# Score products of four key pages, cut into two parts of two pages each, in a one-core decode and prompt step

## The chip, the cores and the metric

One core of a Trainium2 chip. The metric is the device time of one launch in microseconds; lower is better.

## The reference, cut to what matters

One layer of a hybrid decoder for a prompt of 16 + 256 tokens and for 8 decode sequences of 4 new tokens each. Every decode sequence has 2048 past tokens in 16 pages of 128 tokens, in a paged cache of keys and values (float32, 1024 numbers per token each). What the change touches is the product of the queries with the past keys:

```python
q, k, v, u = project_in(xs, l, attn_norm, w_in, q_norm, k_norm)
k_past = cache_k[l][page_table].reshape(db, past_len, 2 * N_HEADS, HEAD_DIM)
v_past = cache_v[l][page_table].reshape(db, past_len, N_HEADS, 2 * HEAD_DIM)
o = diff_attn_core(q, k_all, v_all, q_pos, k_pos, lam)   # softmax over all keys, two maps, values
```

Around it stand the input projection (2048 x 5120), a convolution group, the output projection (2048 x 2048) and an MLP (2048 x 8192 and back), all in float32.

## The kernel before, in words

A weight matrix goes in **visits** of 512 output columns; a visit has 8 chunks of 512 KB (`raw`), which ScalarE rounds to `w_hi` (L1124) and VectorE turns into a rest `w_lo` (L1454). TensorE makes three products of 128x128 tiles for each of 16 row tiles (L691 to L693). The input projection has 10 visits.

**The paged attention runs beside these visits.** Each engine has a program of its own, written out by hand as a `body` of 16 **slots** per decode sequence (the loops over `j`). In the body that works on the keys of sequence `ks` it also works on the values of sequence `vs`, the one before, and on visit `n` of the input projection. There is one body with keys alone (ks=0), then five with keys, values and a visit (ks=1 to 5, called the visit bodies below; the variable `s` of these loops is vs=0 to 4), then two with keys and values beside the prompt's attention and no visit (ks=6 and 7, the free bodies), and a last one for the values of sequence 7. After that come the output projection and the MLP, which is all of the second half of the time.

**A key page's way.** GpSimd (POOL) loads it: `load_keys` (L572 to L579) reads the page number, waits, and issues four DMAs of 128 KB into slot `j % 8` of `k_page`. VectorE transposes it in place in blocks of 32 (`turn`, L1532 to L1536, semaphore `kt_ok`), two slots of the program ahead of need in a visit body (`TURNS`), four ahead in a free body (`FREE_TURNS`). TensorE multiplies a **group** of four pages with the queries of the sequence (`score`, L768 to L780): 8 calls of 512 columns into the one PSUM bank `aux[:, 0]`, then `sc_mm` rises by one. ScalarE copies the bank to `s_rows` (`take_scores`, L1175 to L1181) and raises `s_ev`, which the next group's product waits for. VectorE takes the group's maximum (L1621). At the end of a body come the whole maximum (L1629, L1631), the exponentials on ScalarE (L1218), and in `fresh` (L1609) the next sequence's queries in `q_cur` (L1541) and its products with the new keys in `s_cur` (L1588).

`k_page` has room for 8 pages, so page `j` of a sequence may be loaded only when the page 8 before it has been multiplied. Before, POOL waits for the whole group of four that was two groups earlier. The groups' slots are 3, 7, 11, 15 in a visit body (`SCORES`), 0, 4, 8, 12 in a free body (`FREE_SCORES`), and 5, 10 for groups 2 and 3 of sequence 0 (`FIRST_SCORES`); groups 0 and 1 of sequence 0 come inside visit 3.

On TensorE a slot is, in this order: the group's product if it has one, `new_keys` (L805 to L820, in slot 1 of most bodies), the visit's twelve products of one row tile, `turn_probs` (L792 to L803: transposes of the exponentials of sequence `vs`, slots 0 to 3; the transposes of slots 1 and 3 are copied by VectorE at L1640), and `values` (L822 to L846) of page `j - 2`. The queue of SyncE (SP) loads the chunks of the weights (L392, when TensorE has used an earlier one) and the pages of values (L418, when TensorE has used an earlier one). POOL has three more tasks in between: convolution taps (L619, L621) and outputs (L587, L593, L595) in the fourth visit body and around it, and value outputs (L604).

Of the kernel before, what the change touches and what calls it, by code (L numbers as in the profile page):

```python
# [14 lines left out]
P = 128  # L15
# [5 lines left out]
N_SEQ = 8  # L21
# [14 lines left out]
N_PAGES = 16  # L36
# [9 lines left out]
QD = 32  # L46
NB = P // QD
# [3 lines left out]
SG = 4  # L51
KS = 2 * SG
NG = N_PAGES // SG
# [57 lines left out]
def build_step(nc, x_prompt, x_sample, cache_k, cache_v, state_conv, page_table, meta_tokens,  # L111
# [4 lines left out]
    with ctx:  # L116
# [12 lines left out]
        def sem(name):  # L129
            return ctx.enter_context(nc.semaphore(name))  # L130
# [91 lines left out]
        aux = ctx.enter_context(nc.psum_tensor("aux", [P, 4, 512], F32))  # L222
# [44 lines left out]
        kt_ok = sem("kt_ok")  # L267
        qs_ok = sem("qs_ok")
        qc_ok = sem("qc_ok")
        sc_mm = sem("sc_mm")  # L270
        s_ev = sem("s_ev")
# [85 lines left out]
        def key_rows(r, b):  # L357
            return k_pages[ds(r, 1)].rearrange("a (q x) (b e) -> (a x) q b e", x=KX, b=NB)[:, :, b, :]


        def last_values(i):
            return k_page[:, i % KS].rearrange("p g q c -> p (g q c)")
# [11 lines left out]
        def key_quarter(slot, b):  # L374
            return k_page[QD * b:QD * (b + 1), slot].rearrange("p g q c -> p g (q c)")
# [5 lines left out]
        def _(sp):  # L381
# [15 lines left out]
            def load_last(i):  # L397

                s = N_SEQ - 1
                r = sp.value_load(pages_sb[0:1, ds(N_PAGES * s + i, 1)], min_val=0, max_val=n_phys - 1)  # L400
                src = v_pages[ds(r, 1)].rearrange("a p n -> p (a n)")
                if i >= KS:
                    sp.wait_ge(pv_mm, VR + N_PAGES * s + i - KS + 1)
                elif i < VR:
                    sp.wait_ge(pv_mm, N_PAGES * s + i + 1)
                else:
                    sp.wait_ge(sc_mm, NG * N_SEQ)
                if i % KS < VR:
                    sp.dma_start(v_page[:, i % VR], src).then_inc(v_in[i % VR], 16)
                else:  # L410
                    sp.dma_start(last_values(i), src).then_inc(vk_in[i % VR], 16)
# [57 lines left out]
            for i in range(VR):  # L469
                load_last(i + VR)  # L470
# [2 lines left out]
            for i in range(KS, N_PAGES):  # L473
                load_last(i)

            sp.wait_ge(sc_mm, NG * N_SEQ)
            sp.dma_start(x_nat[:, 0, :], xp[0:P, :]).then_inc(x2_in[0], 16)
            sp.dma_start(x_nat[:, 1, :], xp[P:2 * P, :]).then_inc(x2_in[1], 16)
            sp.wait_ge(pt_mm, NG * N_SEQ)
# [16 lines left out]
            for g in range(4):  # L496
                cols = slice(VC * g, VC * (g + 1))
# [16 lines left out]
        def _(pool):  # L514
# [51 lines left out]
            ks = k_sample[0].rearrange("b t h d -> (b t) (h d)")  # L566
# [5 lines left out]
            def load_keys(s, j, used=True):  # L572

                r = pool.value_load(pages_sb[0:1, ds(N_PAGES * s + j, 1)], min_val=0, max_val=n_phys - 1)  # L574
                slot = j % KS
                if used:
                    pool.wait_ge(sc_mm, NG * s + j // SG - 1)
                for b in (0, 2, 1, 3):
                    pool.dma_start(key_quarter(slot, b), key_rows(r, b)).then_inc(k_in[slot], 16)  # L579

# [91 lines left out]
        def _(pe):  # L672
            mm, transpose = nc.tensor.matmul, nc.tensor.transpose
# [53 lines left out]
            for kt in range(KT):  # L727
# [4 lines left out]
                if kt == 3:  # L732

                    pe.wait_ge(state_in, STATE)
                    for c in range(8):
                        last = transpose(aux[:, 2, TAPS * c:TAPS * (c + 1)], cw_nat[:, P * c:P * (c + 1)],
                                         ident[0:TAPS, 0:TAPS])
# [7 lines left out]
                if kt == 13:  # L745

                    pe.wait_ge(set_v, 14)
                    for t, (t0, n) in enumerate(TOK):
                        last = mm(aux[:, 3, t0:t0 + n], rb[0:n, t, :], ident[0:n, 0:n], start=True, stop=True)
# [15 lines left out]
                    if kt == 3:  # L765
                        norm_sums(n)

            def score(s, g):  # L768

                pe.wait_ge(kt_ok, N_PAGES * s + SG * (g + 1))  # L770
                if g == 0:
                    pe.wait_ge(qc_ok, (NB + 1) * s + NB)
                pe.wait_ge(s_ev, NG * s + g + 2)
                keys = k_page[:, SG * (g % 2):SG * (g % 2 + 1)].rearrange("p j g q c -> p (j g) q c")
                for half in range(2):
                    for c in range(NB):
                        last = mm(aux[QD * c:QD * (c + 1), 0, :].rearrange("p (k c) -> p k c", c=QD),  # L777
                                  q_cur[:, 2 * c + half, :], keys[:, :, 2 * c + half, :],
                                  start=(half == 0), stop=(half == 1))
                last.then_inc(sc_mm, 1)  # L780

            for kt in range(KT):
                products(EARLY, kt, a_hi, a_lo, 0, T)
# [8 lines left out]
            def turn_probs(s, g):  # L792

                pe.wait_ge(exp_ok, (NG + 1) * s + g + 1)
                if g % 2 == 0:
                    pe.wait_ge(pt_d, 1 + 2 * s + g // 2)
                else:
                    pe.wait_ge(pt_a, 2 * s + g // 2 + 1)
                pe.sem_inc(pe_go, 1)
                for j in range(SG):  # L800
                    last = transpose(aux[:, 2, P * j:P * (j + 1)], s_rows[:, P * (SG * g + j):P * (SG * g + j + 1)],  # L801
                                     ident[:])
                last.then_inc(pt_mm, 1)  # L803

            def new_keys(vs, ks):  # L805

                pe.wait_ge(o_ok, (vs if vs is not None else 0) + 1)
                if vs is not None:
                    pe.wait_ge(exp_ok, (NG + 1) * (vs + 1))
                    pe.wait_ge(sel_v, 3 * (vs + 1))  # L810
                    pe.sem_inc(pe_go, 1)
                    mm(aux[0:N_SMP, 3, C_AN:C_AN + 2 * HR], s_rows[:, PAST:PAST + N_SMP],
                       pick_s[:].rearrange("p a c -> p (a c)"), start=True, stop=True)
                    mm(aux[:, 3, C_PV:C_PV + 2 * HR], perm[:].rearrange("p b x c -> p (b x c)"),
                       pick_s[:].rearrange("p a c -> p (a c)"), start=True, stop=True).then_inc(an_mm, 1)
                if ks is not None:
                    pe.wait_ge(qc_ok, (NB + 1) * (ks + 1))
                    pe.sem_inc(pe_go, 1)
                    transpose(aux[:, 3, C_SN:C_SN + N_SMP], s_cur[:].rearrange("p a c -> p (a c)"),
                              ident[0:N_SMP, 0:N_SMP]).then_inc(sn_t, 1)  # L820
# [27 lines left out]
            def body(ks, vs, n, middle=None, end=None, finish=None, new_at=1, scores=SCORES):  # L848


                for j in range(N_PAGES):
                    if ks is not None and j in scores:
                        score(ks, scores[j])
                    if j == new_at:
                        new_keys(vs, ks)
                    if middle:
                        middle(j)
                    if n is not None:
                        products(n, j, a_hi, a_lo, 0, T)
                    if vs is not None and j < NG:  # L860
                        turn_probs(vs, j)
                    if j >= 2 and vs is not None:
                        values(vs, j - 2, ks is not None)
                    if end:
                        end(j)
                if vs is not None:
                    values(vs, N_PAGES - 2, ks is not None)
                    values(vs, N_PAGES - 1, ks is not None)
                    if finish:
                        finish()  # L870

                    pe.wait_ge(or_ok, vs + 1)
                    for a in range(2):
                        last = mm(aux[:, 3, C_EX + HR * a:C_EX + HR * (a + 1)], o_rows[:, P * a:P * (a + 1)],
                                  pick_v[:, a, :], start=True, stop=True)
                    last.then_inc(ex_mm, 1)
# [46 lines left out]
            for t0, n in NAT:  # L923
                for half in range(2):
                    if b >= 4:
                        pe.wait_ge(nat_d if half else nat_a, b // 2 - 1)
                    for h in range(4):
                        last = transpose(acc[0:n, b % 4, P * h:P * (h + 1)],
                                         z[:, 16 + 4 * half + h, PAD + t0:PAD + t0 + n], ident[:])
# [177 lines left out]
            for g in range(4):  # L1107
                pe.wait_ge(acc_free, MT + MT * (MLP_V0 + N_QTR * QTR_N - DOWN_N + g + 1))
                for i, (t0, n) in enumerate(TOK_OUT):
# [3 lines left out]
                    for m in range(MT):  # L1113
                        last = transpose(aux[0:n, b % 4, P * m:P * (m + 1)], xT[:, MT * g + m, t0:t0 + n], ident[:])
# [3 lines left out]
        def _(act):  # L1118
# [55 lines left out]

            def take_scores(ks, g, vs=None):  # L1175

                act.wait_ge(sc_mm, NG * ks + g + 1)
                if vs is not None:
                    act.wait_ge(pt_mm, NG * vs + g + 1)
                nc.scalar.copy(s_rows[:, SG * P * g:SG * P * (g + 1)].rearrange("p (j y g x) -> p j y g x", j=SG, y=KY, g=NB),  # L1180
                               aux[:, 0, :].rearrange("p (j g x y) -> p j y g x", j=SG, g=NB, x=KX)).then_inc(s_ev, 1)  # L1181
# [252 lines left out]
            for b in range(0, 12, 2):  # L1434
                g, i = b // 3, b % 3
# [7 lines left out]
        def _(dve):  # L1443
# [164 lines left out]

            def fresh(ks):  # L1609

                dve.wait_ge(sc_mm, NG * ks)
                dve.wait_ge(sn_t, ks)
                copy_queries(ks)
                copy_new(ks)
# [381 lines left out]
            for b in range(1, 12, 2):  # L1996
                g, i = b // 3, b % 3
# [31 lines left out]
```

## Time and profile before

| what | us |
|---|---|
| median of 3 runs | 1622.88 (1622.68 to 1639.64) |
| the profiled execution, its own time | 1632.08 |
| span of the profiled execution | 1630.4 |
| TensorE busy | 1514.5 (93% of the span) |
| VectorE busy | 975.2 (60%) |
| POOL, DMA issues of the key pages | 332.1, 512 of them |

The profile page is of one execution. Its second section cuts the span into 40 slices of 40.8 us; the keys' loads lie in slices 2 to 16, and from about 690 us on the kernel is the output projection and the MLP. Share of DMA is that of the core's 16 DMA engines.

### The profile page before, as it was taken

The page shows a single profiled execution, that of the slowest core. Times are in us where ns is not written, and L with a number is a line of the kernel's source. Part 1 is how long each engine was busy: PE and PEld are TensorE (multiplying, and loading weights), DVE is VectorE, ACT ScalarE, POOL GpSimd, SP SyncE. Part 2 cuts the span into 40 slices and gives each one's busy share as a digit, 9 for nine tenths or more (in the row PEclk, how much of TensorE's full clock was granted, in tenths as well). Part 3 has the DMA queues.
Part 4 walks back from the last instruction along what each step waited for, and adds up shares of the span by engine and source line. Part 5 has one row for each costly group of instructions (what it writes and reads, how often), then busy time and mean ns, then how long its engine had stood idle before and what let it go on. Part 6 is the DMA issues. An engine that isn't in the chain of part 4 may idle for free.

```text
span 1630.4 us, 31305 instructions
## 1 busy us (share of the span) xinstructions
PE 1514.5 (93%) x11203; PEld 1348.6 (83%) x11203; DVE 975.2 (60%) x1469; ACT 593.8 (36%) x929; POOL 419.7 (26%) x656
## 2 busy tenths in 40 slices
PE   5999898797877868899999999999999999999998
PEld 5988766565654433599999999999999999999998
DVE  3689857998998775353645544455444554445444
ACT  4433312122222332443544433443334433344432
POOL 4597656765787653000000000000000000000000
PEclk9999998998997977799999999999999999999999
DMA  7746799999999776834555545555455545555444
GB/s 201 215 144 185 234 321 333 353 341 327 342 305 349 252 236 221 289 118 154 155 158 165 168 167 162 164 165 166 167 166 162 164 165 167 167 163 163 165 166 148
DMA packets 163845, 340.50 MB, mean 209 GB/s; under 512 B 33915, under 2 KB 33971, under 8 KB 163168
## 3 DMA queue, kind: packets, MB, share of 16 engines
q1 hardware_dynamic: 120592, 267.29, 51.1%
q0 software_dynamic: 43168, 72.15, 14.5%
q8 instruction: 45, 0.74, 0.2%
q14 instruction: 40, 0.33, 0.1%
HBM read 334.00 MB, written 5.96 MB: 209 GB/s over the span
## 4 chain that ended last, share of the span: by engine, by line
PE 72%; issue 10%; DVE 7%; DMA 5%; POOL 3%; POOLq 2%; ACT 1%; SPq 0%; ACTq 0%
PE acc L691 21%; PE acc L693 21%; PE acc L692 21%; DMA k_page<-in_cache_k 3%; PE aux L777 2%; DVE k_page L1536 2%; POOL k_page L579 1%; PE aux L842 1%; POOLq L574 1%; DVE w_lo L1454 1%; DMA raw<-in_w_in 1%; PE acc L945 1%; PE aux L801 1%; POOLq L579 1%; PE acc L965 1%
## 5 line engine op out<-in xcount | busy, mean ns | idle before, releaser
L1454 DVE TENSOR_TENSOR w_lo<-raw,w_hi 128x1024 fp32r<-128x1024 f32 x368 | 451.5, 1229 | 410.2 <-ACT w_hi L1124 409.3
L691 PE MATMUL acc<-a_hi,w_hi 128*128 128x288 f32 (+1 forms) x1920 | 591.8, 308 | 35.2 <-DVE w_lo L1454 26.4
L1124 ACT CAST w_hi<-raw 128x1024 fp32r<-128x1024 f32 x368 | 384.9, 1049 | 586.5 <-DMA raw<-in_w_down 255.4
L693 PE MATMUL acc<-a_hi,w_lo 128*128 128x288 f32 (+1 forms) x1920 | 578.4, 301 | 0.0
L692 PE MATMUL acc<-a_lo,w_hi 128*128 128x288 f32 (+1 forms) x1920 | 578.2, 301 | 0.0
L691 PEld LDWEIGHTS acc<-a_hi,w_hi 128*128 128x128 f32 x1920 | 367.6, 191 | 72.5 <-DVE w_lo L1454 36.5
L579 POOL DMA_DIRECT2D k_page<-in_cache_k x512 | 332.1, 649 | 204.5 <-issue 89.3
L692 PEld LDWEIGHTS acc<-a_lo,w_hi 128*128 128x128 f32 x1920 | 368.3, 192 | 0.5
L693 PEld LDWEIGHTS acc<-a_hi,w_lo 128*128 128x128 f32 x1920 | 368.4, 192 | 0.0
L693 PE MATMUL acc<-h_hi,w_lo 128*128 128x288 f32 x1024 | 302.2, 295 | 0.0
L692 PE MATMUL acc<-h_lo,w_hi 128*128 128x288 f32 x1024 | 301.5, 294 | 0.0
L691 PE MATMUL acc<-h_hi,w_hi 128*128 128x288 f32 x1024 | 301.1, 294 | 0.0
L691 PEld LDWEIGHTS acc<-h_hi,w_hi 128*128 128x128 f32 x1024 | 192.1, 188 | 0.0
L693 PEld LDWEIGHTS acc<-h_hi,w_lo 128*128 128x128 f32 x1024 | 192.1, 188 | 0.0
L692 PEld LDWEIGHTS acc<-h_lo,w_hi 128*128 128x128 f32 x1024 | 192.1, 188 | 0.0
L1536 DVE STREAM_TRANSPOSE k_page<-k_page 128x1024 f32<-128x1024 f32 x128 | 156.8, 1231 | 31.7 <-DMA k_page<-in_cache_k 31.2
L1602 DVE SCALAR_TENSOR_TENSOR conv<-z,taps,conv 128x256 f32<-128x256 f32 x240 | 100.3, 477 | 0.1
L777 PE MATMUL aux<-k_page,q_cur 128*32 128x512 f32 x512 | 70.8, 676 | 20.8 <-DVE k_page L1536 13.8
L1180 ACT COPY s_rows<-aux 128x512 f32<-128x512 f32 x32 | 18.8, 588 | 167.0 <-PE aux L777 167.0
L842 PE MATMUL aux<-v_page,pT 128*16 128x256 f32 x960 | 77.7, 409 | 1.6 <-DMA v_page<-in_cache_v 1.6
L777 PEld LDWEIGHTS aux<-k_page,q_cur 128*32 128x32 f32 x512 | 16.7, 122 | 55.5 <-issue 33.1
L1913 DVE TENSOR_TENSOR xT<-xT,acc 128x288 f32 (+1 forms) x80 | 32.9, 454 | 46.3 <-PE acc L693 46.3
(224 smaller groups left out, 892.6 us busy)
## 6 DMA issues: line engine op xcount, KB each, us to landing
k_page<-in_cache_k POOLq DMA_DIRECT2D x512, 128.0 KB, 6.6
raw<-in_w_up SPq DMA_DIRECT2D x128, 512.0 KB, 3.7
raw<-in_w_down SPq DMA_DIRECT2D x128, 512.0 KB, 3.6
v_page<-in_cache_v SPq DMA_DIRECT2D x120, 512.0 KB, 7.6
raw<-in_w_in SPq DMA_DIRECT2D x80, 512.0 KB, 6.0
raw<-in_w_out SPq DMA_DIRECT2D x32, 512.0 KB, 3.7
k_page<-in_cache_v SPq DMA_DIRECT2D x8, 512.0 KB, 5.5
x_nat<-in_x_prompt SPq DMA_DIRECT2D x3, 1024.0 KB, 8.9
```

The lines of the kernel that those rows point to most:

```text
L579: pool.dma_start(key_quarter(slot, b), key_rows(r, b)).then_inc(k_in[slot], 16)
L691: mm(out, wh, ah, start=(kt == 0), stop=False)
L692: mm(out, wh, al, start=False, stop=False)
L693: last = mm(out, wl, ah, start=False, stop=(kt == KT - 1))
L777: last = mm(aux[QD * c:QD * (c + 1), 0, :].rearrange("p (k c) -> p k c", c=QD), q_cur[:, 2 * c + half, :], keys[:, :, 2 * c + half, :], st ...
L842: last = mm(aux[QD * b:QD * b + HR, 3, 0:2 * P].rearrange("p (a c) -> p a c", a=2), pT[:, b, j, :], page[:, 2 * P * b:2 * P * (b + 1)].rea ...
L1124: nc.scalar.copy(w_hi[:, j % RAW], raw[:, j % RAW]).then_inc(hi_ok, 1)
L1180: nc.scalar.copy(s_rows[:, SG * P * g:SG * P * (g + 1)].rearrange("p (j y g x) -> p j y g x", j=SG, y=KY, g=NB), aux[:, 0, :].rearrange("p ...
L1454: v.tensor_tensor(w_lo[:, j % RAW], raw[:, j % RAW], w_hi[:, j % RAW].bitcast(F32), ALU.subtract)\
L1536: v.transpose(keys, keys).then_inc(kt_ok, 1)
L1602: v.scalar_tensor_tensor(dst, src, w, dst, ALU.mult, ALU.add).then_inc(cv_p, 1)
L1913: v.tensor_tensor(x, x, acc[:, m, 0:T_OUT], ALU.add).then_inc(acc_free, 1)
```

## The change

A group's product is cut in two parts: part 0 multiplies the group's first two pages into the first 256 columns of the bank, part 1 the other two into the last 256. Part 1 stays in the slot of the group, part 0 comes two slots before it (in slot 0 both stand together, since there is no earlier slot; the same in `score`, for groups 0 and 1 of sequence 0). Each part raises `sc_mm` by one, so all waits on it count double. POOL waits for the part that held the page 8 before, no longer for the group.

```diff
-                    sp.wait_ge(sc_mm, NG * N_SEQ)
+                    sp.wait_ge(sc_mm, 2 * NG * N_SEQ)
...
-                    pool.wait_ge(sc_mm, NG * s + j // SG - 1)
+                    pool.wait_ge(sc_mm, 2 * NG * s + (j - KS) // 2 + 1)
...
-            def score(s, g):
-
-                pe.wait_ge(kt_ok, N_PAGES * s + SG * (g + 1))
-                if g == 0:
-                    pe.wait_ge(qc_ok, (NB + 1) * s + NB)
-                pe.wait_ge(s_ev, NG * s + g + 2)
-                keys = k_page[:, SG * (g % 2):SG * (g % 2 + 1)].rearrange("p j g q c -> p (j g) q c")
+            def score_part(s, g, x):
+
+                pe.wait_ge(kt_ok, N_PAGES * s + SG * g + SG // 2 * (x + 1))
+                if x == 0:
+                    if g == 0:
+                        pe.wait_ge(qc_ok, (NB + 1) * s + NB)
+                    pe.wait_ge(s_ev, NG * s + g + 2)
+                j0 = SG * (g % 2) + SG // 2 * x
+                keys = k_page[:, j0:j0 + SG // 2].rearrange("p j g q c -> p (j g) q c")
+                cols = slice(2 * P * x, 2 * P * (x + 1))
                 for half in range(2):
                     for c in range(NB):
-                        last = mm(aux[QD * c:QD * (c + 1), 0, :].rearrange("p (k c) -> p k c", c=QD),
+                        last = mm(aux[QD * c:QD * (c + 1), 0, cols].rearrange("p (k c) -> p k c", c=QD),
                                   q_cur[:, 2 * c + half, :], keys[:, :, 2 * c + half, :],
                                   start=(half == 0), stop=(half == 1))
                 last.then_inc(sc_mm, 1)
+
+            def score(s, g):
+                for x in range(2):
+                    score_part(s, g, x)
...
                 for j in range(N_PAGES):
                     if ks is not None and j in scores:
-                        score(ks, scores[j])
+                        if j == 0:
+                            score_part(ks, 0, 0)
+                        score_part(ks, scores[j], 1)
+                    if ks is not None and j + 2 in scores:
+                        score_part(ks, scores[j + 2], 0)
...
-                act.wait_ge(sc_mm, NG * ks + g + 1)
+                act.wait_ge(sc_mm, 2 * (NG * ks + g + 1))
...
-                dve.wait_ge(sc_mm, NG * ks)
+                dve.wait_ge(sc_mm, 2 * NG * ks)
```

## Rows read from the trace of the kernel before

**Rows 1.** The page's second section: busy tenths in 40 slices, the clock and the DMA.

```profile
POOL 4597656765787653000000000000000000000000
PEclk9999998998997977799999999999999999999999
DMA  7746799999999776834555545555455545555444
```

**Rows 2.** Waits between 60 and 640 us: total, times, longest.

```profile
POOL k_page L579 <- PE aux L777: 71.5, 16, 10.2
DVE k_page L1536 <- DMA k_page<-in_cache_k: 31.2, 28, 3.2
PE aux L777 <- DVE k_page L1536: 12.8, 9, 8.5
DVE w_lo L1454 <- ACT w_hi L1124: 25.0, 14, 5.7
```

**Rows 3.** Windows, one per body: length, engines' busy time, TensorE clock, DMA share, GB/s.

```profile
200.00:262.00 62.00, 51.17 (x407) 36.03 (x405) 34.13 (x46) 14.45 (x26) 38.15 (x60) 0.94 0.99 331
262.00:327.00 65.00, 54.68 (x425) 39.16 (x425) 59.70 (x113) 16.87 (x31) 44.83 (x70) 0.91 1.02 342
327.00:391.50 64.50, 53.98 (x425) 38.09 (x425) 62.74 (x121) 15.40 (x27) 43.22 (x69) 0.92 1.02 345
391.50:458.00 66.50, 54.08 (x426) 38.56 (x426) 62.09 (x113) 17.09 (x31) 44.16 (x70) 0.91 1.00 331
458.00:523.00 65.00, 53.41 (x409) 37.34 (x409) 61.13 (x117) 13.68 (x25) 49.10 (x78) 0.89 0.98 319
523.00:595.00 72.00, 56.89 (x377) 30.44 (x377) 55.65 (x119) 30.49 (x100) 44.94 (x71) 0.85 0.79 256
595.00:645.00 50.00, 42.66 (x252) 19.24 (x252) 31.07 (x74) 15.61 (x62) 23.54 (x37) 0.78 0.78 246
```

**Rows 4.** Windows of 5 us, the same columns.

```profile
185.00:190.00 5.00, 5.00 (x64) 3.32 (x64) 0.62 (x1) 0.27 (x1) 0.25 (x1) 0.94 0.44 114
...
230.00:235.00 5.00, 5.00 (x48) 3.65 (x40) 2.62 (x3) 1.05 (x1) 3.37 (x6) 1.00 1.04 358
```

**Rows 5.** Timeline of POOL: start, length, line, count, in brackets the idle time before and its releaser.

```profile
190.44 1.99 POOL L579 DMA_DIRECT2D k_page<-in_cache_k  x3 [5.19 <-PE aux L777]
...
214.62 2.66 POOL L579 DMA_DIRECT2D k_page<-in_cache_k  x4 [10.24 <-PE aux L777]
217.98 2.66 POOL L579 DMA_DIRECT2D k_page<-in_cache_k  x4 [0.70 <-issue]
...
405.09 2.67 POOL L579 DMA_DIRECT2D k_page<-in_cache_k  x4 [9.68 <-PE aux L777]
...
631.14 2.68 POOL L579 DMA_DIRECT2D k_page<-in_cache_k  x4 [1.76 <-PE aux L777]
```

**Rows 6.** Timeline of TensorE, the same columns.

```profile
204.61 0.22 PE L812 MATMUL aux<-pick_s,s_rows 128*32 128x32 f32 x2 [2.31 <-DVE pick_s L1689]
...
257.51 1.55 PE L842 MATMUL aux<-v_page,pT 128*16 128x256 f32 x24
...
273.78 1.90 PE L777 MATMUL aux<-k_page,q_cur 128*32 128x512 f32 x16
275.61 0.66 PE L913 MATMUL aux<-ident,z 128*128 128x128 f32 x4
...
534.00 3.47 PE L777 MATMUL aux<-k_page,q_cur 128*32 128x512 f32 x16 [2.80 <-DVE s_cur L1588]
537.41 0.66 PE L801 MATMUL aux<-ident,s_rows 128*128 128x128 f32 x4
```

**Rows 7.** Timeline of VectorE, the same columns.

```profile
243.89 1.25 DVE L1536 STREAM_TRANSPOSE k_page<-k_page 128x1024 f32<-128x1024 f32 x1 [3.19 <-DMA k_page<-in_cache_k]
...
265.78 0.86 DVE L1541 COPY q_cur<-q_sel 32x32 f32<-32x32 f32 x4
...
271.31 0.42 DVE L1640 COPY pT<-aux 128x256 f32<-128x256 f32 x1 [2.18 <-PE aux L801]
```

More of the change, by code:

```diff
@@ L474, in _ @@
                 load_last(i)
-            sp.wait_ge(sc_mm, NG * N_SEQ)
+            sp.wait_ge(sc_mm, 2 * NG * N_SEQ)
             sp.dma_start(x_nat[:, 0, :], xp[0:P, :]).then_inc(x2_in[0], 16)
```

## The prediction, made before the changed kernel was run

> **What bounds the kernel now.** I began with the 40 slices. From slice 18 on DMA is at four to five tenths and POOL idle: the second half is weight products and holds no key load [rows 1]. Whatever the change does happens before 690 us, and a gain there shifts the rest of the program as a whole. In slices 7 to 13 DMA shows nine tenths. Next the waits between 60 and 640 us. POOL stood 71.5 us on 16 score products: that is what the change aims at. But the engines that use the pages lost less: VectorE waited 31.2 us for key pages to land, TensorE's scores 12.8 us for VectorE's transposes [rows 2]. So at most some 31 us of POOL's 71.5 is felt downstream directly, and the question is what stands behind.
>
> The windows by body say it. Where DMA is full its share reads 1.04, at 358 GB/s [rows 4]. The first visit body (200 to 262 us) reads 0.99, the others 1.02, 1.02, 1.00 and 0.98 [rows 3]. All five are within 6% of a full DMA. Their bytes are fixed: 16 key pages, 16 value pages and 8 chunks of 512 KB, 40 x 0.524 = 21.0 MB, which takes 59.6 us at 352 GB/s (between the 342 of a body and the 358 of the full window). The bodies take 62 to 66.5 us. In four of them VectorE is busy 60 to 63 of some 65 us besides [rows 3], so both limits lie close under the present time. In the two free bodies DMA reads 0.79 and 0.78, and VectorE 56 of 72 and 31 of 50 us: here neither is full, and the chain of the prompt's attention goes from engine to engine.
>
> **The change part by part.**
>
> *Earlier release of key pages in the visit bodies.* In the first visit body POOL finishes page 7 at 204.4 us and stands 10.24 us until group 0 is done at 213.8 [rows 5]. Part 0 will stand in slot 1, ahead of `new_keys`, whose first product started at 204.61 [rows 6]. I put its end at 206.3, so page 8 is issued at about 207 in place of 214.6, 7.6 us earlier; pages 10 and 11 need part 1, which still ends near 214, and POOL gets there at 207 + 2 x 3.36 = 213.7 (3.36 is 217.98 less 214.62 [rows 5]). So nearly all of the stall goes. The same holds in the other visit bodies (5.99, 7.87 and 9.68 us of stall in the second to the fourth; in the fifth POOL is late by its own taps and outputs and does not stand).
>
> What that is worth is bounded by DMA. If only DMA's unfilled time can be won, that is (1.05 - share)/1.05 x length: 3.5, 1.9, 1.8, 3.2 and 4.3 us, together 14.7 us [rows 3]. I take these terms down where VectorE binds too. First body: VectorE has 34 of 62 us busy and waited there ten times for key pages, 21.4 us in all, of which the row of 243.89 is one [rows 7]; nothing but DMA binds, and ahead of it DMA is far from full (0.44 in 185 to 190 us [rows 4]) while POOL stood 5.19 us for group 3 of sequence 0 [rows 5], whose part 0 moves from slot 10 to slot 8. Filling that moves four pages up by some 4.5 us. I take 5 us here. Second body 1, third 0.5 (VectorE 62.7 of 64.5 busy), fourth 2, fifth 2.5. Sum 11 us. Bounds: 2 us (VectorE's order alone decides after the first body and the first gets only its 2) and 20 us (a whole stall of POOL per body at the places where VectorE waits, 21.4 us in the first and about 7 in the rest, less what DMA refuses).
>
> *Part 0 in slot 1 of a visit body.* It is queued before `new_keys`, the visit's products of that slot, and `turn_probs` of slot 1, for which VectorE waits at L1640 (2.18 us at 271.31 [rows 7]). It needs the queries, ready at 265.78 + 0.86 = 266.64 [rows 7], about when `new_keys` began anyway, and the start of a body is where the clock is down: a group took 3.47 us at 534.00 at 1.2 GHz against 1.90 at full clock [rows 6]. So part 0 puts 1.0 to 1.8 us in front of VectorE's wait. In the second and fourth body VectorE has later waits of the same slots that take most of it up (0.85 and 0.46 us, and 0.86 us); in the third and the fifth there is 0.2 to 0.6 us of slack. At slot 3 TensorE has it back, since part 1 is half a group. Price: 0.5 us a body, 2.5 us in all; bounds 0 and 5 x 1.8 = 9 us.
>
> *More instructions.* A group was 16 recorded matmuls of 512 columns, 1.83 us from its start to the next operation's (275.61 less 273.78 [rows 6]). The rate for 256 columns is that of the value products: 24 in 1.55 us, less a last one of about 0.38, is 0.051 us each [rows 6]. 16 of them are 0.82 us, plus about 0.15 to enter and leave the narrow tiling (8 of them took 0.56 where the rate gives 0.41). Two parts: 1.94 us, +0.11 a group, +3.3 us over 30 groups on an engine that waits at every body's end. I count 0.5 us; bounds 0 and 3.3. The Trainium skill (TensorEngine Tiling (Array Packing), Key Properties) says that changing the tiling mode drains TensorE, and the change doubles the number of such changes; the 0.15 us above is what the trace shows for one, and by it the sum stays as it is.
>
> *The free bodies.* Both parts of group 0 stand in slot 0, but pages 8 and 9 go when part 0 is done: 3.47/2 = 1.7 us earlier. The third stall of length is 6.57 us at 585.5, where VectorE's layer norm of slot 10 held page 15's transpose; part 0 of group 3, in slot 10, needs pages 12 and 13 only and is past that. The last page was issued at 631.14 after stalls of 3.69, 4.66 and 1.76 us in its body [rows 5]; POOL should now reach it 6 to 9 us earlier. Downstream, though, VectorE waited for landings only 0.66, 0.42 and 1.66 us in 534 to 645, and TensorE's one long wait (8.5 us [rows 2]) is for page 15's transpose, which does not move. Gain 2.7 us of landings, plus 1.7 us because at the last group half of the product is done before. Less 1 us for parts put in front of the prompt's products: 3.4 us, say 3. Bounds 0 and 12.
>
> *Waits on `sc_mm` of SP, ScalarE and VectorE* are for the same moment, the end of a group's part 1: nothing. The wait on `s_ev` comes two slots earlier, but ScalarE copies a group 0.6 us after it ends and the next part 0 is two slots away: nothing.
>
> *Sum:* 11 - 2.5 - 0.5 + 3 = 11 us. The profiled execution took 1632.1 us, 9.2 above the median of the runs shown; 1621 against it is 1612 against the median of 1622.9.
>
> **Rivals.**
>
> *POOL's rate is the true bound.* From the first to the fourth visit body each page 8 follows the last by 54 us of issuing and 6 to 10 of standing; the period is that sum. If DMA's full share in the trace is only the queue built up after each late start, then the stalls come off the period: 10 + 6 + 8 + 10 less the 2.5 us above, and 6 of the free bodies' 27, some 35 us at most. Against it stand 59.6 us of bytes per body and a busy VectorE. As a case I take 25 us: 1598.
>
> *It is hidden almost wholly.* VectorE binds from the second body on, and the free bodies wait on the prompt's chain. Then only the first body's 4 us less 2 to 3 us of part 0 remains: 1621. For it: busy times of 60 to 63 us. Against: VectorE waited for key landings near the end of each of these bodies, and again for the weights.
>
> *Slower: keys in front of weights.* At a body's start TensorE waits for `w_lo`, VectorE for `w_hi` (25.0 us, 14 times [rows 2]), ScalarE for raw chunks. Now key pages and the chunks of slots 2 to 4 are loaded at one time, where before POOL stood. If four DMAs of keys (two pages, 1.05 MB, 3 us at 352 GB/s) come before a chunk, VectorE's order slips by up to 3 us in a body that it binds; with the 1.8 us of part 0 that is 4.8 us x 5 = 24, less the 11: 13 us slower, 1636. It decides if the chunk's landing was the last thing VectorE waited for at the body's start, which it was in three bodies by 0.85 to 1.75 us. The Trainium skill (DMA: Bandwidth & Descriptors, Queues, rings and completion order) states that each DMA engine takes turns between the queues that have work, packet by packet. By that rule a chunk loses part of its rate while keys are queued, not its whole place; this leaves the rival with half its price. No row shows single packets here.
>
> **How the numbers follow.** Forecast (about 11 us, own range 1605 to 1618): 0.50. POOL's rate (1598): 0.20. Hidden (1621): 0.22. Slower (1636): 0.08. The range 1597 to 1624 leaves out the slower case and the end of the POOL case. One per cent, 16.2 us, is about what a measurement of this kernel can tell from no change. Faster by more than that (under 1606.7) is the POOL case and a little of the forecast's upper end: 0.26. Slower by more is the outer half of the last rival: 0.05. Within 1%: 0.69.
>
> **What would show it.** Right: POOL's wait for L777 falls from 71.5 to under 25 us; in the first visit body page 8 is issued near 207 and VectorE's waits for landings, 21.4 us, fall by a third or more; DMA shares of the visit bodies go to 1.03 and over; bodies of 60 to 64 us; the score of a part near 1.0 us at full clock; the last score about 11 us earlier and everything after it unchanged in length. The POOL rival: bodies under 59 us. The hidden rival: POOL's wait gone and bodies two to five the same. The slower one: more time of ScalarE on `raw` and of VectorE on `w_hi` in slots 2 to 4, or on L801. The forecast is wrong if the bodies after the first do not shorten, or if a new stall of POOL on later parts takes the old one's place with the same length.

## The result, and the profile of the changed kernel

| what | before | changed |
|---|---|---|
| median of 20 runs, us | 1626.57 (1621.71 to 1639.64) | 1617.35 (1615.61 to 1622.91) |
| profiled execution, span, us | 1630.4 | 1615.0 |

The ratio is 0.994, 95% interval 0.9926 to 0.9954: 9.2 us faster by the medians. In the comparisons below the ratios leave out one run of `early_both` and one of the kernel before beside it, which took several times as long as the rest. The two profiled spans differ by 15.4 us, more than the medians; part of that is chance, as a second trace of the kernel before shows below.

The page's second section, against [rows 1]: the work of the first third is packed a little closer, the second half is the same.

```profile
POOL 4498667766776752000000000000000000000000
PEclk9999999998988969799999999999999999999999
DMA  7656899999999868645555555555555555555554
```

The waits between 60 and 640 us, against [rows 2] (total, times, longest; L781 is now the score product, L1548 the transpose, L850 the product with the values, L1652 the copy of transposed probabilities):

```profile
ACT w_hi L1136 <- DMA raw<-in_w_in: 101.7, 35, 6.8
...
POOL k_page L579 <- PE aux L781: 52.2, 15, 12.6
...
DVE w_lo L1466 <- ACT w_hi L1136: 27.1, 16, 4.6
...
PEld aux L850 <- DMA v_page<-in_cache_v: 22.3, 13, 3.3
PE aux L781 <- DVE k_page L1548: 20.4, 22, 8.0
...
PE aux L850 <- DMA v_page<-in_cache_v: 16.7, 11, 2.8
...
DVE pT L1652 <- PE aux L809: 11.7, 6, 4.4
...
DVE k_page L1548 <- DMA k_page<-in_cache_k: 9.3, 5, 2.5
```

POOL's wait for scores fell only from 71.5 to 52.2 us; in the five visit bodies alone it fell from 37.3 (200 to 523 us) to 31.4 (200 to 514 us). VectorE's wait for key pages fell from 31.2 to 9.3. What is new is TensorE waiting for **value** pages: 13 waits, 22.3 us, at the weight loads and 16.7 at the matmuls of much the same stops; before there were 5, of 3.6 us in all. ScalarE's wait for chunks of the weights (`raw`) rose too, from 76.7 us in 24 waits to 101.7 in 35. Keys that come earlier are paid for with values and weights that come later.

Windows by body, against [rows 3]. Body ends are read at the last small product of a body, which before stood at 262.3, 327.1, 391.6, 457.9, 523.3, 594.9 and 660.0 us and now at 261.1, 323.4, 386.6, 451.1, 513.8, 587.2 and 639.1.

```profile
200.00:261.00 61.00, 50.37 (x460) 36.61 (x458) 32.77 (x45) 16.90 (x34) 38.88 (x60) 0.93 0.97 324
261.00:323.40 62.40, 53.06 (x489) 39.34 (x489) 58.80 (x113) 14.23 (x21) 44.70 (x70) 0.94 1.05 354
323.40:386.60 63.20, 53.16 (x489) 38.56 (x489) 62.48 (x120) 15.65 (x27) 43.19 (x67) 0.93 1.05 352
386.60:451.00 64.40, 53.11 (x489) 39.24 (x489) 60.42 (x112) 16.79 (x31) 44.28 (x71) 0.92 1.03 346
451.00:513.80 62.80, 52.90 (x473) 37.74 (x473) 61.17 (x119) 14.27 (x25) 48.43 (x77) 0.91 0.98 325
513.80:587.20 73.40, 59.80 (x440) 33.87 (x440) 55.36 (x118) 31.59 (x102) 45.20 (x71) 0.81 0.86 271
587.20:639.00 51.80, 44.98 (x389) 22.89 (x389) 35.05 (x87) 19.55 (x79) 20.72 (x32) 0.93 0.76 248
```

The second to the fourth visit body now have DMA at 1.05, 1.05 and 1.03, where it was 1.02, 1.02 and 1.00; 1.05 is the highest share that any of these traces reads over a body. They are 62.4, 63.2 and 64.4 us long, the fifth 62.8 at an unchanged 0.98. The first visit body ended only 1.2 us earlier, and its share is 0.97. In windows of 5 us, against [rows 4]:

```profile
205.00:210.00 5.00, 5.00 (x29) 4.38 (x22) 1.66 (x2) 0.00 (x0) 2.59 (x4) 0.50 0.82 293
210.00:215.00 5.00, 5.00 (x47) 4.06 (x46) 2.12 (x6) 1.48 (x3) 2.59 (x4) 0.87 0.81 245
215.00:220.00 5.00, 5.00 (x48) 4.02 (x50) 5.00 (x6) 2.31 (x3) 3.67 (x6) 1.00 0.74 219
```

DMA is still not full from 205 to 220 us, and no fuller than before: the kernel before read 1.05, 0.75 and 0.63 in the same three windows, 0.81 in the mean beside 0.79 now (0.93 and 0.69 in the second traces, below). What was filled lies ahead of them: 185 to 190 us read 0.44 before and 0.61 now, 190 to 195 us 0.58 and 0.89. POOL's timeline, against [rows 5], says when pages 8 and 10 of that body and page 8 of the next were issued:

```profile
206.80 2.66 POOL L579 DMA_DIRECT2D k_page<-in_cache_k  x4 [8.10 <-PE aux L781]
...
215.55 2.66 POOL L579 DMA_DIRECT2D k_page<-in_cache_k  x4 [2.73 <-PE aux L781]
...
267.91 2.66 POOL L579 DMA_DIRECT2D k_page<-in_cache_k  x4 [3.08 <-PE aux L781]
```

Page 8 came at 206.8, as forecast (207), in place of 214.6; the stall was 8.10 us all the same, because POOL had been brought forward in the body before (it had finished page 7 at 198.7 us in place of 204.4). TensorE's and VectorE's timelines at the same place, against [rows 6] and [rows 7]:

```profile
204.27 1.78 PE L781 MATMUL aux<-k_page,q_cur 128*32 128x256 f32 x16 [3.11 <-issue]
205.74 0.32 PE L820 MATMUL aux<-pick_s,s_rows 128*32 128x32 f32 x2
```

```profile
272.49 1.05 PE L781 MATMUL aux<-k_page,q_cur 128*32 128x256 f32 x16
273.47 0.66 PE L925 MATMUL aux<-ident,z 128*128 128x128 f32 x4
```

```profile
211.09 0.42 DVE L1652 COPY pT<-aux 128x256 f32<-128x256 f32 x1 [4.44 <-PE aux L809]
...
240.45 1.25 DVE L1548 STREAM_TRANSPOSE k_page<-k_page 128x1024 f32<-128x1024 f32 x1 [2.55 <-DMA k_page<-in_cache_k]
...
253.20 1.25 DVE L1548 STREAM_TRANSPOSE k_page<-k_page 128x1024 f32<-128x1024 f32 x1 [2.00 <-DMA k_page<-in_cache_k]
```

A part takes 1.78 us in slot 1, where the clock is down, and 1.05 us at full clock, 0.98 to the start of the next operation (forecast 1.0 at full clock and 1.7 at the start of a body). `new_keys` comes 1.1 us later, and VectorE's first wait for transposed probabilities is 4.44 us where it was 1.85 in that body.

### The profile page after: what moved, and what is told of

Same layout as the page of the kernel before. It is cut to its first block, busy times and chain, and to the rows that moved or that the text cites. A ratio compares the mean times of both kernels' runs of the same rounds, so it can differ in the third digit from the quotient of the medians.

```text
span 1615.0 us, 32337 instructions
## 1 busy us (share of the span) xinstructions
PE 1507.7 (93%) x11715; PEld 1357.5 (84%) x11715; DVE 972.6 (60%) x1469; ACT 595.8 (37%) x929; POOL 420.5 (26%) x656
## 4 chain that ended last, share of the span: by engine, by line
PE 76%; DVE 18%; DMA 3%; issue 1%; ACT 1%; POOL 1%; SPq 0%; POOLq 0%; ACTq 0%
PE acc L691 22%; PE acc L693 21%; PE acc L692 21%; DVE conv L1614 6%; DVE k_page L1548 5%; DVE w_lo L1466 3%; PE aux L781 2%; PE aux L850 2%; DMA v_page<-in_cache_v 1%; PE acc L957 1%; PE acc L977 1%; PE aux L809 1%; DMA raw<-in_w_in 1%; DVE s_max L1633 1%; DVE z L1584 1%
## 5 line engine op out<-in xcount | busy, mean ns | idle before, releaser
L1548 DVE STREAM_TRANSPOSE k_page<-k_page 128x1024 f32<-128x1024 f32 x128 | 156.2, 1229 | 9.3 <-DMA k_page<-in_cache_k 9.3
L781 PE MATMUL aux<-k_page,q_cur 128*32 128x256 f32 x1024 | 72.4, 406 | 31.2 <-DVE k_page L1548 20.4
L850 PE MATMUL aux<-v_page,pT 128*16 128x256 f32 x960 | 78.9, 410 | 16.7 <-DMA v_page<-in_cache_v 16.7
L781 PEld LDWEIGHTS aux<-k_page,q_cur 128*32 128x32 f32 x1024 | 31.5, 114 | 63.3 <-DVE k_page L1548 32.5
```

Source lines behind the costliest of these rows:

```text
L781: last = mm(aux[QD * c:QD * (c + 1), 0, cols].rearrange("p (k c) -> p k c", c=QD), q_cur[:, 2 * c + half, :], keys[:, :, 2 * c + half, :], ...
L850: last = mm(aux[QD * b:QD * b + HR, 3, 0:2 * P].rearrange("p (a c) -> p a c", a=2), pT[:, b, j, :], page[:, 2 * P * b:2 * P * (b + 1)].rea ...
L1548: v.transpose(keys, keys).then_inc(kt_ok, 1)
```

## The experiments

Each ratio is to the kernel before, timed on the same chip. The column of the visit bodies is the distance from the first body's end to the fifth's in the trace of the run: the time that the change is about, free of what comes before and after. The last column is from the fifth body's end to the end of the last body.

| kernel | median, us | ratio (95%) | first body ends | visit bodies 2 to 5 | free and last bodies |
|---|---|---|---|---|---|
| before | 1626.57 | 1 | 262.3 | 261.0 | 164.3 |
| before_trace | 1619.65, one run | | 260.3 | 261.7 | 152.5 |
| changed | 1617.35 | 0.994 (0.9926 to 0.9954) | 261.1 | 252.8 | 158.4 |
| again_after | 1618.2 | 0.9926 (0.9901 to 0.995) | 264.2 | 253.0 | 157.7 |
| group_release | 1628.14 | 0.9991 (0.9971 to 1.0011) | 264.4 | 259.7 | 160.3 |
| same_slot | 1626.4 | 0.9973 (0.9947 to 0.9999) | 262.3 | 261.4 | 160.7 |
| late_first_part | 1622.74 | 0.9956 (0.9932 to 0.998) | 261.9 | 256.3 | 160.8 |
| visit_only | 1615.67 | 0.9925 (0.99 to 0.995) | 262.8 | 252.8 | 154.1 |
| free_only | 1628.04 | 1.001 (0.9988 to 1.0032) | 262.2 | 260.8 | 159.7 |
| early_queries | 1618.56 | 0.9928 (0.9904 to 0.9951) | 262.6 | 257.5 | 158.2 |
| early_both | 1624.79 | 0.9983 (0.9955 to 1.0011) | 258.3 | 258.7 | 161.2 |
| half_values_before | 1612.17 | 0.9883 (0.9822 to 0.9943) | 257.4 | 251.7 | 156.6 |
| half_values_after | 1609.13 | 0.9873 (0.9818 to 0.9929) | 253.8 | 253.6 | 158.6 |

**The two kernels once more.**

> The changed kernel once more, as the yardstick for the runs beside it: ratio to before 0.994 +- 0.002, as in the first measurement. Its trace should show again that the visit bodies end some 9 us earlier than before and tell how much of the free bodies' shift (13 us less in the second, 6 more in the last) is the clock of TensorE and not the change.

> The kernel before once more, for a second trace: the first one was 5 us above its median. If TensorE's half clock between 605 and 620 us was chance, the second free body ends 3 to 8 us earlier here and the difference to the changed kernel's trace at 640 us falls from 21 to some 10 us.

The changed kernel repeats itself: 253.0 us for the four bodies against 252.8. The second trace of the kernel before has a span of 1618.0 us, below all its timed medians; its visit bodies take 261.7 us, as in the first, but its free and last bodies are 11.8 us shorter. Its second free body ended 14.0 us earlier (646.0 beside 660.0 us), where 3 to 8 had been expected. Windows of the first trace (16 us) and then of the second (5 us each, the first and the last of four; all four read 1.00), the last columns being TensorE's clock, DMA's share and GB/s:

```profile
600.00:616.00 16.00, 16.00 (x80) 8.72 (x76) 9.76 (x26) 4.74 (x19) 10.36 (x16) 0.61 0.73 205
```

```profile
600.00:605.00 5.00, 4.83 (x35) 3.45 (x37) 4.02 (x11) 2.51 (x10) 4.25 (x8) 1.00 0.48 128
...
615.00:620.00 5.00, 4.02 (x30) 1.86 (x30) 4.90 (x11) 1.74 (x8) 3.69 (x7) 1.00 0.93 304
```

The first trace ran that stretch at a clock of 0.61 of full speed in the mean, the second at 1.00. The kernel was the same. So the last column of the table carries some 10 us of chance, a single pair of traces says nothing on the free bodies, and the 13 us that the second free body seemed to win are mostly this. By the five bodies' end the two traces of the kernel before stood at 523.3 and 522.1 us, those of the changed kernel at 513.8 and 517.2: 4.9 to 9.5 us, with the 9.2 of the medians inside. The spread comes from the end of the first visit body; the four bodies after it agree within 1 us from trace to trace of a kernel. That holds for their sum and not for a single one: the second body took 64.8 and 62.2 us in the two traces of the kernel before.

What the four bodies gain shows at VectorE. Its waits for key pages to land came there to 7.1 and 5.3 us in the two traces of the kernel before; in both traces of the changed kernel there is none. That is most of the 8 us.

**The release alone, and the lead alone.**

> The products stay in two parts at the new places, but POOL waits for whole groups again. Theory (the gain is the earlier release of pages): no gain is left and part 0 still stands in front of the body's start, so 0 to 3 us slower than before, ratio 1.000 to 1.002. Rival (the gain is that part 1 is only half a group on TensorE's path): most of the gain stays, ratio 0.995 to 0.997.

```diff
-                    pool.wait_ge(sc_mm, 2 * NG * s + (j - KS) // 2 + 1)
+                    pool.wait_ge(sc_mm, 2 * (NG * s + j // SG - 1))
```

> Both parts in the group's own slot, POOL waits for parts. Pages 8 and 9 are released 1 us earlier than in the kernel before and not 7 to 8. Theory (two slots of lead carry the gain): about before, ratio 0.998 to 1.000. Rival (release by halves is enough): ratio 0.994 to 0.996.

```diff
                     if ks is not None and j in scores:
-                        if j == 0:
-                            score_part(ks, 0, 0)
-                        score_part(ks, scores[j], 1)
-                    if ks is not None and j + 2 in scores:
-                        score_part(ks, scores[j + 2], 0)
+                        score(ks, scores[j])
```

With the products split and placed as in the change but the pages released by groups, nothing is left of the gain: 0.9991, visit bodies 259.7 us, and 4.6 us of waits for landings in them are back. So it does not come from a shorter last product on TensorE's path. Nor does TensorE's clock tell the kernels apart: over the first 16 us of each of the four bodies it was 0.82 in the mean here, 0.83 and 0.75 in the two traces of the kernel before, 0.84 in the changed kernel. Its windows are those of the kernel before [rows 3]; DMA's shares are back at 1.02, 1.03, 1.00 and 0.98; the second and the fourth body:

```profile
264.40:327.60 63.20, 52.76 (x490) 39.12 (x490) 59.25 (x112) 16.86 (x31) 43.46 (x68) 0.93 1.02 339
...
391.80:457.70 65.90, 53.62 (x490) 39.37 (x490) 61.05 (x112) 16.85 (x31) 44.30 (x71) 0.91 1.00 332
```

Nor does it show a cost of the 8 further matmul calls per group: the interval, 0.9971 to 1.0011, holds no change. With release by halves but no lead (`same_slot`) the visit bodies take 261.4 us with 6.6 us of waits for landings, as before; the ratio, 0.9973, lies a little under the range set down (0.998 to 1.000) and its interval ends just under 1, so a gain of some microseconds outside these bodies is not ruled out. For the visit bodies both halves of the change are needed: the product must come earlier and POOL must be let go by it.

**Where in the program.**

> The two free bodies work as before (both parts in the group's slot, POOL waits for whole groups for their pages), the visit bodies as in the changed kernel. The forecast's terms put 8 of 11 us into the visit bodies: with 9.5 us measured, 7 us faster than before, ratio 0.995 to 0.9965. If the free bodies carry the gain, as the two profiles side by side could be read (13 us less in the second free body), ratio 0.998 to 1.000.

> The counterpart: visit bodies as before, free bodies as in the changed kernel. Forecast's terms: 2 to 3 us faster than before, ratio 0.998 to 0.999. If the free bodies carry the gain: 7 us or more, ratio under 0.996.

In these two, `body` calls `score` for the bodies that stay as before, and `load_keys` waits by groups for the pages that those bodies set free. All of the gain is in the visit bodies (0.9925, 252.8 us; more than the 7 us expected), none in the free ones (1.001, where 0.998 to 0.999 was expected). `visit_only` has the lowest median of the kernels that do all the work, but its interval is that of the changed kernel; the two were not timed on one chip, and I don't call it faster. POOL did gain time in the free bodies of the changed kernel, as its timeline shows:

```profile
592.85 2.67 POOL L579 DMA_DIRECT2D k_page<-in_cache_k  x4 [12.63 <-PE aux L781]
```

POOL runs ahead through sequence 6 and then stands 12.63 us before page 8 of sequence 7, whose part 0 needs that sequence's queries, and these come at the body's end. The stalls of 6.57 and 3.69 us before pages 4 and 8 became one, those of 4.66 and 1.76 us before pages 12 and 15 went. The last page was issued 29.7 us after the start of its body (616.88 less 587.2), 6.5 us sooner than before (631.14 less 594.9), and in the trace of `free_only` VectorE never waits for a landing in the free bodies, where the kernel before did for 2.7 and 3.8 us in its two traces. So the pages came earlier as forecast and the time did not follow: they were not what these bodies waited for. What is, these runs don't show.

**Part 0 in front of the body's start.**

> Part 0 of group 0 in the visit bodies goes behind the products and the transposes of slot 1, so VectorE's first wait for transposed probabilities is as before, while pages 8 and 9 are released some 4 us later than in the changed kernel. If part 0 in front costs what the forecast took (0.5 us a body) or more and POOL's release is not the limit: 1 to 5 us faster than the changed kernel, ratio 0.991 to 0.9935. If the release time rules: 1 to 4 us slower than it, ratio 0.9945 to 0.9965.

```diff
                     if vs is not None and j < NG:
                         turn_probs(vs, j)
+                    if ks is not None and vs is not None and j == 1 and j + 2 in scores:
+                        score_part(ks, scores[j + 2], 0)
```

(and the call ahead of the products is left out for that slot.) The release time rules: 0.9956, visit bodies 256.3 us, 3.5 more than in the changed kernel. Page 8 was issued 2.8 to 5.7 us later after the start of its body than in the changed kernel (second to fourth visit body). Its waits, in the columns of above:

```profile
POOL k_page L579 <- PE aux L781: 62.7, 19, 13.0
...
DVE k_page L1550 <- DMA k_page<-in_cache_k: 17.6, 8, 3.8
...
DVE pT L1654 <- PE aux L809: 8.0, 5, 2.4
```

VectorE's waits for transposed probabilities went back from 11.7 to 8.0 us, so part 0 does cost what stands in front of it, 3.7 us in all; but POOL's wait rose by 10.5 us and VectorE's for landings by 8.3. These microseconds of earlier release are worth more than the price.

**An attempt at both.**

> On top of the change, VectorE copies the next sequence's queries before the last maximum of a visit body, and TensorE makes part 0 of the next group 0 at the body's end, where it idles 3 to 6 us for VectorE, and no longer in slot 1. Pages 8 and 9 are released 6 to 8 us earlier and nothing stands in front of slot 1's transposes. If the start of the body holds what the change left (part 0 in front of VectorE's wait, POOL still standing 3 to 9 us): 3 to 6 us faster than the changed kernel, ratio 0.990 to 0.992. If DMA and VectorE bind for the whole body: no difference from it, ratio 0.994.

```diff
+                if ks is not None and ks < PAIR_V:
+                    dve.wait_ge(sc_mm, 2 * NG * (ks + 1))
+                    copy_queries(ks + 1)
                 if ks is not None and maxes is not FREE_MAXES:
                     group(NG - 1)
...
                     values(vs, N_PAGES - 1, ks is not None)
+                if ks is not None and ks < PAIR_V:
+                    score_part(ks + 1, 0, 0)
```

(Cut here: for these bodies the call in slot 1 and the copy of the queries in `fresh` are left out.)

> As early_queries, and part 1 of group 0 goes from slot 3 to slot 2 of a visit body: in early_queries POOL stood 6 to 8 us for part 1 (page 10) in place of part 0. If POOL's release at the body's start is worth time: its stall there falls under 4 us and the kernel is 2 to 4 us faster than early_queries, ratio 0.990 to 0.992. If DMA and VectorE hold the bodies, or the half clock at the start of a body does: no difference, ratio 0.992 to 0.994.

```diff
+                    if ks is not None and j == 2 and scores is SCORES:
+                        score_part(ks, 0, 1)
```

(Cut here: the call in slot 3 is left out.)

Neither beats the change. `early_queries` has the ratio of the second comparison of the change, 0.9928, so of the two answers set down for it the second holds, no difference. Its trace, with visit bodies of 257.5 us, is of its slowest run (1622.73 us, median 1618.56). There POOL's stall moved from page 8 to page 10, which waits for part 1 (first line, POOL), and VectorE's wait for the transposes of slot 1 did not shrink but grew, to 5.54 us (second line, VectorE):

```profile
276.90 2.66 POOL L579 DMA_DIRECT2D k_page<-in_cache_k  x4 [5.71 <-PE aux L781]
```

```profile
272.60 0.42 DVE L1656 COPY pT<-aux 128x256 f32<-128x256 f32 x1 [5.54 <-PE aux L809]
```

TensorE's clock is a likely cause. Windows of the first 16 us of the second and the fourth body, of `early_queries` and then of the changed kernel's second trace:

```profile
262.50:278.50 16.00, 16.00 (x104) 14.44 (x101) 9.54 (x21) 4.70 (x9) 8.61 (x14) 0.70 1.05 336
392.10:408.10 16.00, 16.00 (x105) 14.28 (x105) 10.08 (x22) 6.95 (x17) 6.70 (x11) 0.70 0.83 260
```

```profile
264.20:280.20 16.00, 15.98 (x127) 13.57 (x128) 12.42 (x29) 5.39 (x10) 10.00 (x16) 0.84 1.05 342
389.90:405.90 16.00, 15.97 (x124) 13.39 (x125) 12.19 (x28) 7.52 (x19) 7.13 (x11) 0.82 0.94 303
```

The clock was 0.70 in the mean in both where the changed kernel had 0.84 and 0.82. The fifth body, where `early_queries` had the higher clock (0.86 beside 0.81), is its only one that was shorter (61.1 beside 62.8 us). Whether the product moved into TensorE's idle time lowers the clock, or chance does, these runs don't tell: the kernel before, too, read 0.69 to 0.70 at the start of three of these bodies in one trace and 0.82 to 0.87 in the other.

`early_both` has a ratio of 0.9983 (0.9955 to 1.0011), above the range set down for either answer and above the interval of `early_queries`; the two were not timed on one chip. POOL's stalls before page 10 did fall, from 6.52, 5.71, 5.98 and 7.63 us in the first four visit bodies to 3.55, under 1, 5.28 and 2.56, and the kernel was not faster, so releasing page 10 earlier did not pay.

**DMA relieved.**

> The kernel before, but all value pages of sequences 0 to 6, except the first four, are loaded with half of their columns (the other half of the output uses what the buffer held): 26 MB less through DMA, every instruction of the engines the same. Theory (POOL's stalls and VectorE, not DMA, set the bodies before): little faster, 0 to 6 us, ratio 0.996 to 1.000. If DMA's bytes set the bodies already before: 12 us or more, ratio under 0.993.

> The changed kernel with the same half loads. Theory (in the changed kernel DMA's bytes hold the visit bodies, most of all the first one, where TensorE now waits for value pages): 8 us or more faster than the changed kernel, so the change is worth 12 to 20 us against half_values_before, ratio to before 0.982 to 0.988. If VectorE or the start of the body holds them: at most 3 us faster than the changed kernel, ratio 0.991 to 0.994.

```diff
-                sp.dma_start(v_page[:, slot], v_pages[ds(r, 1)].rearrange("a p n -> p (a n)")).then_inc(v_in[slot], 16)
+                n = D_ATTN if isinstance(s, int) and s == 0 and i < VR else D_ATTN // 2
+                sp.dma_start(v_page[:, slot, 0:n], v_pages[ds(r, 1)].rearrange("a p n -> p (a n)")[:, 0:n]).then_inc(v_in[slot], 16)
```

By the count of pages 28 MB are left out (108 pages, 0.26 MB each; the expectation said 26). This tells what the change pays in, by four runs of each kernel. The kernel before wins 17 us by the loads alone (1612.17 beside 1629.57; in the traces 4.9 us up to the end of the first visit body and 9.3 in the four after it), and its waits for landings in the four bodies are gone, so its bodies were held by bytes; of the two answers set down for it, the one I had called the theory was the wrong one. And once DMA is relieved the change is worth 3 us by the medians (1609.13 beside 1612.17), inside both intervals, and not 12 to 20: in the visit bodies two to five it is worth nothing, 253.6 against 251.7 us. The changed kernel itself ends 8 to 9 us earlier with the half loads (1617.35 and 1618.2 to 1609.13, on different chips), as set down, and its ratio to the kernel before, 0.9873, lies in the range given; but the time went in its first visit body (253.8 us where it had 261.1 and 264.2) and not in the next four, which stay at 253. So after the change bytes still hold the program up to the end of the first visit body, and no longer the other four. Windows of `half_values_before`, the second and the fourth body, and two of its waits:

```profile
257.40:318.80 61.40, 51.87 (x426) 36.87 (x426) 59.06 (x112) 16.72 (x31) 45.92 (x72) 0.95 0.95 294
...
381.50:447.70 66.20, 55.88 (x426) 40.42 (x426) 61.19 (x112) 16.84 (x31) 44.17 (x70) 0.89 0.80 247
```

```profile
POOL k_page L580 <- PE aux L778: 56.0, 16, 10.2
...
DVE k_page L1537 <- DMA k_page<-in_cache_k: 16.2, 8, 3.5
```

POOL still stands 56.0 us for scores here, 15.3 of them in the four bodies, and none of it makes VectorE wait for a page there: DMA is at 0.80 to 0.95, and VectorE is busy 59 to 62 of 61 to 66 us. With the change, with half the values and with both, the four bodies take 252 to 254 us. That VectorE, the busiest engine there, sets this floor is argued from its busy time; no run made its work less. The first body is the exception: 257.4 with half the values, 253.8 with the change on top, where with all values it ended between 258 and 264 us in every kernel.

## Why the prediction was right, and where its terms were not

**The sum came out, in part by luck.** Forecast 11 us, measured 9.2 by the medians and 12 by the ratio of the second comparison (0.9926), inside the forecast's own range and within 1%, the case with the highest chance. The mechanism, an earlier release of key pages by a part that stands earlier, is what `group_release` and `same_slot` show. But the gain lies elsewhere than the terms put it, and errors of opposite sign made up for each other.

**The limit was named, and it is two limits.** The forecast said that DMA's unfilled time bounds the gain and that VectorE binds close behind. Shares of 1.05, 1.05 and 1.03, and the kernel with whole groups released (shares and time back as before), agree with the first; the fifth body, though, gained 2.7 us in the first pair of traces at an unchanged share of 0.98. The half loads show where DMA stops being the limit: once the change is in, fewer bytes no longer shorten the bodies two to five.

**The rivals.** That of POOL's rate (25 us) is refuted: the visit bodies are held at 62 to 64 us with 31 us of POOL's stalls still in them. That of a gain almost wholly hidden, with bodies two to five the same, is out by their 8 us. Of the slower one the signs were there, VectorE's wait for `w_hi` rising from 25.0 to 27.1 us and ScalarE's for `raw` from 76.7 to 101.7, and the price was not.

**The first body's term failed** (5 us). Page 8 came at 206.8, as worked out, and VectorE's waits for landings fell from 21.4 to 9.3 us, but the body's end did not move beyond chance (262.3 and 260.3 us before, 261.1 and 264.2 now): TensorE's products then waited 6.8 us for value pages, where they had not waited, and VectorE 6.4 us for `w_hi`, where it had been 1.7. The step that failed is that DMA's gap at the body's start would be filled by keys. It was filled ahead of the body; from 205 to 220 us DMA's share was 0.79 in the mean and had been 0.81, since SP's queue also waits there for TensorE, which part 0 had made later: the weights' chunk issued at 208.49 us before came at 210.24, the value pages of 212.32 at 214.11. Only with half the values did the end move, by 4.9 us, and by 8.5 with the change on top (2.9 and 6.5 against the second trace of the kernel before).

**The bodies two to five were mis-sized the other way.** Terms of 1, 0.5, 2 and 2.5 us, less 0.5 for each, make 4; measured 8.0 to 8.9 (261.0 and 261.7 against 252.8 and 253.0). The third body, of which I expected nothing because VectorE was busy 62.7 of 64.5 us, gave 1.3 in the first pair of traces; the others gave 2.5, 1.8 and 2.7. The free bodies' 3 us were not there: `free_only` shows 1.001. So two terms, 5 and 3, were wrong, and a third that was half its size made up for them.

**The price of part 0** was about right: 2.5 us forecast, 3.7 us of more waiting at VectorE, by the difference to `late_first_part`. A group in two parts takes 2 x 0.98 = 1.96 us where it took 1.83, as worked out (1.94); what that costs the kernel (0.5 us forecast) can't be told from nothing.

**POOL's wait** was to fall under 25 us and fell to 52.2. One of the two signs that were to show the forecast wrong did come in part: in the first visit body new stalls of 8.10 and 2.73 us stand in place of 10.24, in the fourth 8.96 in place of 9.68. The other, that the bodies after the first don't shorten, did not. The first of these was no sign of the time: POOL, let go earlier, comes earlier to the next thing it has to wait for, and what counts is when the page lands against when VectorE wants it.

## What to carry to other kernels

A stall on a loading queue is worth at most what the DMA engines lose by it, and nothing if nobody waits for its data: before counting it, read the share of DMA in the same stretch, take unfilled share times length as the bound, and look for the waits for landings of the engine that uses the data. Here these waits in bodies two to five, 5 to 7 us against none, told the kernel before from the changed one better than the queue's own wait, 27 us against 21 to 23. When DMA is full, an earlier load of one kind delays another, and the wait moves to whoever uses the second kind. Halving one load once shows whether bytes still hold a stretch, and so how much any better order of the loads can still bring.

## What the runs showed of the hardware that I had not expected

TensorE's clock differs between two executions of one program by enough to hide a change of this size: 0.61 against 1.00 of full speed over the same 16 us of the free bodies, in traces that took 164.3 and 152.5 us from the fifth body's end to the last one's. Splitting a product of 16 recorded matmuls of 512 columns (1.83 us a group at full clock) into two parts of 16 with 256 columns made it 1.96 us, and cost nothing that the timed runs can tell.
